# A decoder layer on one core: input normalised in pairs of tiles, first projections interleaved with the transposes

## The reference

```python
hn = rms_norm(x, norm_mix_pre)
proj = hn @ w_in                       # 1024 x 2560: lru_x, lru_gate, q, k, v, 512 each
y_lru = rglru_group(lru_x, lru_gate, ...)   # conv over 4 taps, sigmoid gates, scan over tokens
y_att = diff_attn_group(q, k, v, ...)       # 4 heads, each the difference of two softmaxes
x = x + rms_norm(concat(y_lru, y_att) @ w_out, norm_mix_post)
hm = rms_norm(x, norm_mlp_pre)
x = x + rms_norm(relu(hm @ w_up) ** 2 @ w_down, norm_mlp_post)
```

## Time and profile before

| | |
|---|---|
| median of 3 runs | 1272.79 us (1269.55 to 1273.96) |
| the profiled execution | 1270.29 us, span 1268.5 us |
| mean granted clock of TensorE | 0.969 of full |
| PE busy | 1185.9 us, 93% of the span |
| DVE, ACT, POOL busy | 634.6, 410.1, 57.9 us |

### The profile page before, as it was taken

How to read it: one execution, slowest core, us unless ns; L and a number is a source line. 1 busy time by engine, 2 the same in 40 slices (tenths; PEclk the granted TensorE clock), 3 DMA queues, 4 the chain that set the end, 5 groups by cost and what they waited for, 6 DMA issues and landing times.

```text
span 1268.5 us, 13563 instructions
## 1 busy us (share of the span) xinstructions
PE 1185.9 (93%) x5232; PEld 954.9 (75%) x5232; DVE 634.6 (50%) x815; ACT 410.1 (32%) x671; POOL 57.9 (5%) x37
## 2 busy tenths in 40 slices
PE   4999799988888899968999999999999999999997
PEld 3888678865566678757888888888888888888885
DVE  6655754445556555474444444354444444443546
ACT  7434721134556444653112112211221121122122
POOL 0000000000002012040000000000000000000014
PEclk9999899987888999989999999999999999999998
DMA  5111243320010042222111102110111111011102
GB/s 202 57 33 50 69 155 95 95 83 17 0 67 1 1 163 86 74 92 83 38 45 50 50 33 66 50 50 33 66 50 44 39 50 50 33 66 50 51 34 116
DMA packets 22081, 78.86 MB, mean 62 GB/s; under 512 B 2800, under 2 KB 2928, under 8 KB 21920
## 3 DMA queue, kind: packets, MB, share of 16 engines
q1 hardware_dynamic: 17504, 63.45, 14.8%
q0 software_dynamic: 2720, 10.68, 2.4%
q10 hardware_dynamic: 1824, 4.29, 1.5%
HBM read 67.92 MB, written 6.29 MB: 59 GB/s over the span
## 4 chain that ended last, share of the span: by engine, by line
PE 84%; DVE 8%; ACT 4%; issue 3%; DMA 1%; DVEq 0%; SPq 0%; ACTq 0%
PE pair L294 25%; PE pair L296 25%; PE pair L295 25%; PE pair L519 4%; PE pair L549 3%; DVE negmax L1218 1%; DVE wl L1056 1%; DVE xl L1095 1%; PE pair L522 1%; DMA x_sb<-x 1%; PE pair L534 1%; DMA yacc<-x 1%; PE pair L583 1%; PE pair L413 1%; DVE probs L1212 0%
## 5 line engine op out<-in xcount | busy, mean ns | idle before, releaser
L294 PE MATMUL pair<-yh,wh 128*128 128x512 f32 x512 | 200.8, 392 | 15.1 <-DVE wl L1056 15.1
L1353 DVE TENSOR_TENSOR yacc<-yacc,pair 128x1024 f32<-128x1024 f32 x112 | 136.7, 1220 | 133.0 <-PE pair L296 133.0
L295 PE MATMUL pair<-yl,wh 128*128 128x512 f32 x512 | 200.4, 391 | 0.0
L296 PE MATMUL pair<-yh,wl 128*128 128x512 f32 x512 | 200.4, 391 | 0.0
L295 PE MATMUL pair<-wdl,xh 128*128 128x512 f32 x480 | 187.0, 390 | 0.0
L294 PE MATMUL pair<-wdh,xh 128*128 128x512 f32 x480 | 187.0, 390 | 0.0
L296 PE MATMUL pair<-wdh,xl 128*128 128x512 f32 x480 | 186.8, 389 | 0.0
L1341 DVE TENSOR_TENSOR relu<-relu 128x512 f32<-128x512 f32 x64 | 44.3, 692 | 216.3 <-ACT xh L990 216.3
L1056 DVE TENSOR_TENSOR wl<-raw,wh 128x1024 fp32r<-128x1024 f32 x74 | 93.5, 1265 | 75.8 <-ACT wh L727 75.8
L294 PEld LDWEIGHTS pair<-yh,wh 128*128 128x128 f32 x512 | 96.9, 189 | 36.0 <-DVE wl L1056 11.5
L727 ACT ACTIVATE wdh<-raw 128x1024 fp32r<-128x1024 f32 x30 | 30.3, 1054 | 279.7 <-PE pair L296 274.4
(11 more groups left out here) (178 smaller groups left out, 1496.8 us busy)
## 6 DMA issues: line engine op xcount, KB each, us to landing
raw<-weights SPq DMA_DIRECT2D x104, 512.0 KB, 3.3
x_sb<-x SPq DMA_DIRECT2D x4, 1024.0 KB, 10.3
q_rot<-q_sb ACTq DMA_DIRECT2D x32, 128.0 KB, 2.3
out<-h_sb SPq DMA_DIRECT2D x7, 512.0 KB, 2.6
y_spill<-gel POOLq DMA_DIRECT2D x4, 512.0 KB, 3.1
lru_raw<-y_spill POOLq DMA_DIRECT2D x1, 2048.0 KB, 9.5
x_a<-x POOLq DMA_DIRECT2D x4, 512.0 KB, 5.2
yacc<-x POOLq DMA_DIRECT2D x1, 2048.0 KB, 8.4
```

Of the source, the lines that this page charges most:

```text
L294: pe.matmul(o, a_hi, b_hi, start=first, stop=False)
L295: pe.matmul(o, a_hi, b_lo, start=False, stop=False)
L296: return pe.matmul(o, a_lo, b_hi, start=False, stop=last)
L1353: dve.tensor_tensor(y, y, pair[2 + t % 2][:, :], ALU.add).then_inc(y_added, 1)
```

## The change

In the changed kernel

- x comes in eight transfers of 512 KB, weight piece 0 between the fourth and the fifth tile and piece 1 behind the last;
- ACT makes a Sqrt on one column of ones first, and then all eight squares; means and roots are taken per pair of tiles (four times), and DVE scales two tiles after each;
- PE transposes the first token half in two rounds of 16 (tiles 0 and 1, tiles 2 and 3, all eight banks);
- then PE runs s = 0 over the first token half, into bank 0; then, for each k, the four transposes of the second half (banks 4 to 7 in turn) followed by the three matmuls of s = 1 over the first token half, into bank 2; then bank 1 (s = 0, second half), bank 3 (s = 1, second half), and the gate products of c = 0. The loop goes from c = 1;
- ACT and DVE have the squares, roots, scalings and splits written out in an order of their own.

The diff, without the declarations of semaphores (`x_loaded` becomes eight, `squares_v` goes) and without blank lines:

```diff
@@ -338,11 +337,11 @@
         @block.sync
         def _(sp):
-            for i in range(4):
-                sp.dma_start(x_sb[:, 2 * i:2 * i + 2, :],
-                             x[0].rearrange("(t p) d -> p t d", p=P)[:, 2 * i:2 * i + 2, :]).then_inc(x_loaded[i], 16)
-            for s in range(2):
-                sp.dma_start(raw[s][:, :], weights[s]).then_inc(raw_loaded[s], 16)
+            for t in range(TT):
+                if t == TT // 2:
+                    sp.dma_start(raw[0][:, :], weights[0]).then_inc(raw_loaded[0], 16)
+                sp.dma_start(x_sb[:, t, :], x[0, P * t:P * t + P, :]).then_inc(x_loaded[t], 16)
+            sp.dma_start(raw[1][:, :], weights[1]).then_inc(raw_loaded[1], 16)
             with sp.Fori(0, PIECES // 2 - 1) as i:
                 for s in range(2):
                     sp.wait_ge(w_lo, 2 * i + s + 1)
@@ -448,27 +447,15 @@
             pe.wait_ge(ident_loaded, 32)
-            for hf in range(2):
-                pe.wait_ge(scaled, 4 * (hf + 1))
+            for q in range(2):
+                pe.wait_ge(scaled, 2 * q + 2)
                 for k in range(KC):
-                    if hf == 1:
-                        pe.wait_ge(tr_lo, k + 1)
-                    transposes([x_sb[:, 4 * hf + t, P * k:P * k + P] for t in range(4)], k)
-
-            with pe.Fori(0, LC) as c:
-                for s in range(2):
-
-
-                    pe.wait_ge(w_lo, 2 * c + s + 1)
-                    if s == 0:
-                        pe.wait_ge(tr_lo, KC + 1)
-                    for hf in range(2):
-                        if s == 0 and hf == 1:
-                            pe.wait_ge(tr_lo, 2 * KC)
-                        mm = feature_bank(s, pair[s][:, HALF * hf:HALF * hf + HALF], xh, xl, hf)
-                    mm.then_inc(piece_used, 1)
-
-
+                    for t in range(2 * q, 2 * q + 2):
+                        mm = pe.transpose(bank(k)[:, P * t:P * t + P], x_sb[:, t, P * k:P * k + P], ident[:, :])
+                    if q == 1:
+                        mm.then_inc(tr_done, 1)
+
+            def gate_products(c):
                 pe.wait_ge(xc_lo, c + 1)
                 for g in range(2):
                     for hf in range(2):
@@ -476,6 +463,30 @@
                         mm = mm3(pe, pair[2 + g][:, tok], gwh[:, g, :], gwl[:, g, :], xch[:, tok],
                                  xcl[:, tok], True, True)
                     mm.then_inc(gates_done, 1)
+
+            pe.wait_ge(w_lo, 1)
+            feature_bank(0, bank(0), xh, xl, 0, 0)
+            pe.wait_ge(w_lo, 2)
+            pe.wait_ge(scaled, TT)
+            for k in range(KC):
+                if k >= 4:
+                    pe.wait_ge(tr_lo, KC + k - 3)
+                transposes([x_sb[:, 4 + t, P * k:P * k + P] for t in range(4)], 4 + k % 4)
+                mm3(pe, bank(2), pieces_of(wh[1])[:, k, :], pieces_of(wl[1])[:, k, :], xh[:, k, 0:HALF],
+                    xl[:, k, 0:HALF], k == 0, k == KC - 1)
+            feature_bank(0, bank(1), xh, xl, 1, KC).then_inc(piece_used, 1)
+            feature_bank(1, bank(3), xh, xl, 1).then_inc(piece_used, 1)
+            gate_products(0)
+
+            with pe.Fori(1, LC) as c:
+                for s in range(2):
+
+
+                    pe.wait_ge(w_lo, 2 * c + s + 1)
+                    for mm in feature_piece(s, pair[s], xh, xl):
+                        pass
+                    mm.then_inc(piece_used, 1)
+                gate_products(c)
             pe.wait_ge(lru_copied, 2 * LC)
             pe.wait_ge(sig_done, 2 * LC)
@@ -734,21 +745,6 @@
             act.dma_start(ident[:, :], constants[0]).then_inc(ident_loaded, 16)
             act.dma_start(cols[:, :], columns).then_inc(ident_loaded, 16)
-            n_sq = 0
-            for t in range(TT):
-                if t % 4 < 3:
-                    if t % 2 == 0:
-                        act.wait_ge(x_loaded[t // 2], 16)
-                    if n_sq >= 2:
-                        act.wait_ge(squares, n_sq - 1)
-                    act.activation(u_t[:, n_sq % 2, :], x_sb[:, t, :], ACT.Square,
-                                   accum_out=mean_sq[:, 0, t:t + 1]).then_inc(squares, 1)
-                    n_sq += 1
-                else:
-                    act.wait_ge(var_ready, t // 4 + 1)
-                    act.activation(root[:, t - 3:t + 1], var[:, t - 3:t + 1], ACT.Sqrt).then_inc(root_ready, 1)
-            hi_early(0)
-            act.wait_ge(ident_loaded, 32)
             def split_hi(n, dst, gain0, b):
@@ -757,9 +753,41 @@
                 act.activation(dst[:, k, HALF * hf:HALF * hf + HALF], bank(b), ACT.Copy,
                                scale=cols[:, gain0 + k:gain0 + k + 1]).then_inc(tr_hi, 1)
-            for n in range(2 * KC):
-                split_hi(n, xh, C_GPRE, n % KC)
+            def x_square(t):
+                act.wait_ge(x_loaded[t], 16)
+                if t >= 2:
+                    act.wait_ge(squares, t - 1)
+                act.activation(u_t[:, t % 2, :], x_sb[:, t, :], ACT.Square,
+                               accum_out=mean_sq[:, 0, t:t + 1]).then_inc(squares, 1)
+
+            def x_root(q):
+                act.wait_ge(var_ready, q + 1)
+                act.activation(root[:, 2 * q:2 * q + 2], var[:, 2 * q:2 * q + 2], ACT.Sqrt).then_inc(root_ready, 1)
+
+            def x_high(first, last):
+                for n in range(first, last):
+                    split_hi(n, xh, C_GPRE, n if n < KC else 4 + n % 4)
+
+            act.wait_ge(const_ready, 1)
+            act.activation(root[:, 0:1], ones[:, 0:1], ACT.Sqrt)
+            for q in range(2):
+                x_square(2 * q)
+                x_square(2 * q + 1)
+                x_root(q)
+            hi_early(0)
+            act.wait_ge(ident_loaded, 32)
+            x_square(4)
+            x_high(0, 3)
+            x_square(5)
+            x_high(3, 4)
+            x_root(2)
+            x_high(4, 6)
+            x_square(6)
+            x_high(6, KC)
+            x_square(7)
+            x_root(3)
             hi_early(1)
+            x_high(KC, 2 * KC)
             act.wait_ge(small_loaded, 32)
             act.activation(ident_r[:, :], ident[:, :], ACT.Copy)
             act.activation(mask_r[:, :], mask_raw[:, :], ACT.Copy).then_inc(act_step, 1)
@@ -1072,21 +1100,21 @@
             dve.memset(ones[:, :], 1.0).then_inc(const_ready, 1)
-            for gq in range(2):
-                sl = slice(4 * gq, 4 * gq + 4)
-                dve.wait_ge(x_loaded[2 * gq + 1], 16)
-                t = 4 * gq + 3
-                dve.tensor_tensor_reduce(out=u_t[:, 2 + gq, :], in0=x_sb[:, t, :], in1=x_sb[:, t, :], scale=1.0,
-                                         scalar=0.0, op0=ALU.mult, op1=ALU.add,
-                                         accum_out=mean_sq[:, 0, t:t + 1]).then_inc(squares_v, 1)
-                dve.wait_ge(squares_v, gq + 1)
-                dve.wait_ge(squares, 3 * gq + 3)
-                rsqrt_pre(mean_sq[:, 0, sl], var[:, sl], D, var_ready)
-                dve.wait_ge(root_ready, gq + 1)
+            def x_var(q):
+                dve.wait_ge(squares, 2 * q + 2)
+                rsqrt_pre(mean_sq[:, 0, 2 * q:2 * q + 2], var[:, 2 * q:2 * q + 2], D, var_ready)
+
+            def x_scale(q):
+                sl = slice(2 * q, 2 * q + 2)
+                dve.wait_ge(root_ready, q + 1)
                 rsqrt_post(var[:, sl], root[:, sl], t1[:, sl], t2[:, sl], rstd[:, 0, sl])
-                for t in range(4 * gq, 4 * gq + 4):
+                for t in range(2 * q, 2 * q + 2):
                     dve.tensor_scalar(x_sb[:, t, :], x_sb[:, t, :], rstd[:, 0, t:t + 1], None,
                                       ALU.mult).then_inc(scaled, 1)
+
+            for q in range(2):
+                x_var(q)
+                x_scale(q)
             def split_lo(n, dst_h, dst_l, gain0, b):
                 hf, k = divmod(n % 16, KC)
@@ -1096,11 +1124,21 @@
                                          dst_h[:, k, cols_].bitcast(F32), ALU.mult,
                                          ALU.subtract).then_inc(tr_lo, 1)
+            def x_low(first, last):
+                for n in range(first, last):
+                    split_lo(n, xh, xl, C_GPRE, n if n < KC else 4 + n % 4)
+
             lo_early(0)
             dve.wait_ge(ident_loaded, 32)
-            for n in range(2 * KC):
-                split_lo(n, xh, xl, C_GPRE, n % KC)
+            x_low(0, 3)
+            x_var(2)
+            x_low(3, 4)
+            x_scale(2)
+            x_low(4, KC)
+            x_var(3)
+            x_scale(3)
             lo_early(1)
+            x_low(KC, 2 * KC)
             dve.wait_ge(small_loaded, 32)
             link(dve.tensor_scalar(head_gain[:, :], cols[:, C_HEADG:C_HEADG + 1], 1.0 - LAM_INIT, None, ALU.mult))
```

More of the change, by code:

```diff
@@ L179, in sem @@
             return ctx.enter_context(nc.semaphore(name))
-        x_loaded = [sem(f"x_loaded{i}") for i in range(4)]
+        x_loaded = [sem(f"x_loaded{i}") for i in range(TT)]
```

(1 more changed line is left out.)

## The result

| | before | changed |
|---|---|---|
| median, 10 runs each | 1272.44 us (1269.55 to 1276.94) | 1279.06 us (1273.0 to 1283.53) |
| ratio, 95% interval | | 1.0049 (1.0029 to 1.0068) |
| the profiled execution | 1270.29 us | 1279.35 us |

The account below looks back on a forecast made before the run. The start was taken as bound by DVE's chain through tiny string, copy and convolution to gates(0). The earlier first half (-2.4) and new order net +3.7, plus 1.7 of clock: 1272.8 + 5.4 = 1278.2 us, range 1271.5 to 1283.

Parts of the forecast that it names:

- First half scaled: Start of the kernel: first token half completely scaled at 14.4 instead of 16.8 us, a gain of 2.4.
- Start of the interleaved steps: PE's interleaved transposes and products start at 27.8 us, when DVE's queue has finished the low part of weight piece 1.
- Clock in those steps: Interleaved steps: low PE clock after idling costs between nothing and 1.7 us, 0.9 taken.
- Copy: ACT's copy of u_t ahead of the first convolution: at 45.6 us, behind the tiny string on DVE.
- gates(0): First gate products, c = 0: start at 55.35 us, 3.7 later than the 51.62 of before.
- The clock at the gates: PE idles 6.7 us ahead of gates(0), so they start at 1.2 GHz: +1.7 us.
- Sum at c = 1: Products of c = 1: start 5.4 us later than before, from +3.7 for gates(0) plus 1.7 of clock.
- C: Rival: gates(0) come right behind bank 3 at full clock; -3.8, 1269.0 us; chance 0.07.
- D: Rival: nothing changes, within 1 us, as the copy waits for bank 1, not the tiny string; chance 0.06.
- E: Rival: smaller transfers slower, or clock low through all gates and start of c = 1; +9 and more, 1282 up; chance 0.07.
- B: Rival: same mechanism, small: DVE without waits, loop at full clock, half the clock cost at gates; +2.9, 1275.7; chance 0.20.
- case A: Main case, 0.60: later gates(0) plus low clock there; from +4 to +8, 1276.6 to 1281; own range also given as 1275.5 to 1281.5.

Follow-up runs that it names:

- e3: Changed kernel plus 26 matmuls that nobody reads, between bank 3 and the gate products; ratio to before 1.0038 (1.0024 to 1.0052).
- e8: Changed kernel without the first Sqrt on ones; profiled once, not timed; second convolution's xcl starts at 78.83 us.
- e2: Changed kernel with the tiny string and its Exp moved behind the first convolution's low parts; ratio to before 1.0040 (1.0026 to 1.0053).
- e7: Changed kernel with x in four transfers of 1 MB again; executed once, no ratio; second convolution's xcl starts at 81.78 us.
- e10: Same kernel as e8 (changed kernel without the first Sqrt), now timed; ratio to before 1.0061 (1.0040 to 1.0082).
- e4: Changed kernel with second-half transposes in one go, then bank 1 first, and the tiny string behind the first convolution; ratio to before 0.9975 (0.9960 to 0.9991).
- e9: Changed kernel, but PE makes all transposes first, then banks 0 to 3; executed once, no ratio; second convolution's xcl starts at 76.08 us.
- e1: Changed kernel with only PE's order changed: second-half transposes in one go, then bank 1 first; ratio to before 0.9997 (0.9981 to 1.0013).

## Why the prediction was right

Step by step, changed kernel, forecast and measured:

- First half scaled: 14.4, 14.2. Table load out of the path and tile 3 in time, both seen.
- Start of the interleaved steps: 27.8, 27.50, at the end of DVE's queue.
- Clock in those steps: 0.9 taken, between 0 and 1.7. The steps started 1.73 and 2.14 apart and then 1.13; the eighth began at 37.05 instead of 27.50 + 7 x 1.13 = 35.4, so 1.65 in this execution.
- Copy: 45.6, 46.27, released by the string. gates(0): 55.35, 55.98. PE's wait: 6.7, 6.75.
- **The clock at the gates is the term that was mis-sized:** 1.7 forecast from the 3.8 us of the earlier trace rows, 2.9 measured (e3 against the changed kernel, 78.35 against 81.24). The low clock lasted 6.2 us behind the restart here, over all twelve gate products and the first products of c = 1. The error was to take one stall's 3.8 us as a fixed length: behind waits of 3.6 to 6.8 us here the price was 1.4 (e8), 2.5 (e2, e7), 2.8 (e10) and 2.9.
- Sum at c = 1: +5.4 forecast, +7.25 by the marker; the timed difference is 6.6 in medians, 6.2 by the ratio (3.7 to 8.7). The mechanism is the one forecast. That the median came within 1 us of 1278.2 is in part luck, since both terms of the clock vary from one execution to the next by as much as that.

Of the rivals, C (gates at PE's own pace) needed exactly what e4 builds: there gates(0) come right behind bank 3, and the gain is 0.25%. In the changed kernel the order of banks forbids it. D fell, since the copy was released by the string, and e2's copy moves once the string is out of its way. Of E, the slower transfers fell with e7. Its other condition, all gates and the start of c = 1 at 1.2 GHz, came about in the profiled execution, but it cost 2.9 and not the 5 that E's +9 needs. B was too mild on every term in that execution; e2, e8 and e10 do show its interleaved steps at full clock, and e8 a price at the gates below the 1.7. The text gives case A two ranges, from +4 to +8 and 1275.5 to 1281.5; the result lies in both.

Three pieces of the change can be priced at the marker, each from two single executions and with whatever the clock did in them. The new front with the old order of banks costs 2.1 (e9), about 1 of it the clock. Bank 0 ahead of the second half's transposes gives back 2.2 (e1 against e9). Interleaving bank 2 with those transposes, and waiting for weight piece 1 ahead of them, costs 7.35 (e1 against the changed kernel), of which 6.1 stand at gates(0) and 1.3 are the clock behind them; only this third piece is larger than what the clock can do by itself. It costs that much since it fills PE with products that nobody waits for, while the copy waits for bank 1 and for the string, which stands behind the last low part.

## What to carry to other kernels

Ask of each product moved forward who waits for it: PE's idle time in the beginning was filled, and what filled it pushed back the one result on which a serial chain of 10 us hung. Cost the chain from its release to the next instruction in the busy engine's order, and charge a new wait of some microseconds twice on PE, once for itself and once for the clock behind it. And where single executions scatter by more than the effect, compare the traces at an instruction shortly behind the change.

## What the runs showed of the hardware

- Behind a wait of 2.4 us the clock came to 1.2 GHz (e1), though it fell only after PE had started again (1.00 in the stretch from 49 to 50, 0.50 from 51 to 52); one of 1.97 us in before left it at 1.00.
- A wait of the same length doesn't always do it. Ahead of the interleaved steps PE waits 2.6 us in the changed kernel, e3, e7 and e2. In the first three the clock fell to 0.50 over those steps, in e2 it stayed at 1.00.
- How long it then stays low, counted from PE's restart, varies: 2.9 us in e8, 3.8 in the earlier trace rows, 4.3 in e1, 6.0 in e10, 6.2 in the changed kernel. e8 and e10 are the same program, behind the same wait of 6.76 us.
- Most of the scatter lies in attention. From the marker to the first `diag`, which stands behind attention, the same instructions took 364.2 us in before, 365.4 in the changed kernel, 368.2 in e1, 361.6 in e7 and 370.4 in e8 (365.3 in e10, the same program), with a mean granted clock from 0.91 to 0.93. Up to attention's first product on `probs` these executions agree within 0.3 us:

```profile
73.99:438.20 364.21, 328.18 (x1448) 0.93 0.18 58
```

```profile
78.83:449.20 370.37, 335.53 (x1448) 0.91 0.18 57
```

That is more than the whole change moves, and it is why the total of one execution would have misled here: e8's was 1281.4, with a marker 2.4 ahead of the changed kernel's.
